# Attention scores as two 64-row matmuls per pair of heads, issued by pairs, with the middle blocks unrolled

## What is computed

```python
sc = jnp.einsum("bhrqd,bhrkcd->bhrqkc", qg, kb) * (hd ** -0.5)       # A: 4 heads, 8 x 16 neighbourhood
sc = jnp.where(col_valid[:, None, :], sc + bias, NEG_INF)
p = jax.nn.softmax(sc.reshape(b, h, rows, GRID_W, kr * GRID_W), axis=-1)
...
o, lse = banded_attention(q, k, v, half_w, slopes, dilation, sink)   # B: 6 heads, +-128 tokens, sink
...
for window, d in ((128, 1), (512, 4), (2048, 16)):                   # C: 6 heads, three dilations,
    o, lse = banded_attention(to_sub(q), to_sub(k), to_sub(v), ...)  #    merged by their denominators
```

## Time and profile before

| what | value |
|---|---|
| median of 3 runs | 2898.84 us (2894.78 to 2903.01) |
| span of the profiled execution | 2891.3 us |
| PE busy | 2779.0 us, 96% |
| DVE busy | 1347.7 us, 47% |
| ACT busy | 862.7 us, 30% |
| granted TensorE clock, mean | 0.989 of full |
| attention, first layer | 287.6 to 605.5 us |
| attention, second layer | 1717.6 to 2035.6 us |

### The profile page before, as it was taken

The page is one execution under the profiler, slowest core; times in us unless marked ns, Lnnn a source line. Parts: engine busy times, 40 slices in busy tenths (PEclk is TensorE's granted clock), DMA queues, the critical chain, the costliest instruction groups (busy, mean ns, idle before and its releaser), DMA issues.

```text
span 2891.3 us, 38682 instructions
## 1 busy us (share of the span) xinstructions
PE 2779.0 (96%) x13768; PEld 2299.5 (80%) x13768; DVE 1347.7 (47%) x2898; ACT 862.7 (30%) x1688; POOL 152.3 (5%) x254
## 2 busy tenths in 40 slices
PE   5999999989999999999989999999899999999998
PEld 5877888777888888888878778878778888888886
DVE  4377666663233333333434776666542333333333
ACT  3222655543211111111032236555441111111110
POOL 2000311100000000000000003111000000000000
PEclk9999999999999999999999999999999999999999
DMA  5211600021111111111041125000212111111111
GB/s 161 77 44 48 155 30 12 17 94 44 57 46 51 44 51 51 44 51 44 0 138 44 44 81 125 19 18 12 104 33 66 51 44 51 44 50 46 48 37 58
DMA packets 212196, 161.44 MB, mean 56 GB/s; under 512 B 52976, under 2 KB 190192, under 8 KB 212080
## 3 DMA queue, kind: packets, MB, share of 16 engines
q1 hardware_dynamic: 204176, 159.93, 18.4%
q10 hardware_dynamic: 7904, 0.04, 0.2%
HBM read 137.27 MB, written 22.66 MB: 55 GB/s over the span
## 4 chain that ended last, share of the span: by engine, by line
PE 45%; DVE 3%; ACT 1%; issue 1%; DVEq 0%; POOL 0%; POOLq 0%; ACTq 0%
PE psum L1433 11%; PE psum L1435 11%; PE psum L1434 11%; PE psum L1519 4%; PE psum L1555 3%; PE psum L1535 2%; PE psum L1484 1%; PE psum L1449 1%; ACT UH L325 0%; DVE X L1313 0%; DVE XN L947 0%; DVE GL L1303 0%; DVE TA L1192 0%; DVE GT L1300 0%; DVE T L1044 0%
## 5 line engine op out<-in xcount | busy, mean ns | idle before, releaser
L1433 PE MATMUL psum<-HH,UH 128*128 128x512 f32 x1856 | 743.1, 400 | 1.3 <-ACT VB L725 1.3
L1435 PE MATMUL psum<-HH,UL 128*128 128x512 f32 x1856 | 723.0, 390 | 0.0
L1434 PE MATMUL psum<-HL,UH 128*128 128x512 f32 x1856 | 723.0, 390 | 0.0
L329 DVE TENSOR_TENSOR UL<-UR,UH 128x1024 fp32r<-128x1024 f32 x116 | 142.0, 1227 | 852.3 <-ACT UH L325 852.3
L1433 PEld LDWEIGHTS psum<-HH,UH 128*128 128x128 f32 x1856 | 348.5, 188 | 86.7 <-issue 12.0
L1434 PEld LDWEIGHTS psum<-HL,UH 128*128 128x128 f32 x1856 | 348.5, 188 | 83.4 <-issue 12.0
L1435 PEld LDWEIGHTS psum<-HH,UL 128*128 128x128 f32 x1856 | 348.4, 188 | 72.7
L1313 DVE TENSOR_TENSOR X<-X,psum 128x512 f32<-128x512 f32 x352 | 236.0, 685 | 147.4 <-PE psum L1435 146.7
L1433 PE MATMUL psum<-PH,GH 128*128 128x512 f32 x704 | 276.0, 392 | 3.0 <-DVE X L1313 3.0
L1434 PE MATMUL psum<-PL,GH 128*128 128x512 f32 x704 | 274.1, 389 | 0.0
L1435 PE MATMUL psum<-PH,GL 128*128 128x512 f32 x704 | 274.0, 389 | 0.0
(11 more groups left out here) (143 smaller groups left out, 3168.3 us busy)
## 6 DMA issues: line engine op xcount, KB each, us to landing
UR<-in_w_gu SPq DMA_DIRECT2D x176, 256.0 KB, 3.1
PR<-in_w_down SPq DMA_DIRECT2D x88, 256.0 KB, 2.9
UR<-in_w_in SPq DMA_DIRECT2D x56, 256.0 KB, 3.2
x_res<-X SPq DMA_DIRECT2D x2, 4096.0 KB, 13.5
PR<-in_w_out SPq DMA_DIRECT2D x32, 256.0 KB, 4.5
X<-x_res SPq DMA_DIRECT2D x2, 4096.0 KB, 14.2
G<-g_d SPq DMA_DIRECT2D x32, 198.0 KB, 2.5
VR<-v_c SPq DMA_DIRECT2D x16, 390.0 KB, 3.6
```

What stands on the lines that cost most here:

```text
L329: nc.vector.tensor_tensor(UL[:, slot, :, :], UR[:, slot, :, :], UH[:, slot, :, :].bitcast(F32), ALU.subtract).then_inc(unit_lo, 1)
L1433: t.matmul(dst, sh, mh, start=start, stop=False)
L1434: t.matmul(dst, sh, ml, start=False, stop=False)
L1435: return t.matmul(dst, sl, mh, start=False, stop=stop)
```

## The change

- `score` becomes `score_pair`: the scores of tiles s and s + 1 are issued together. Each multiplies over 64 rows only, the lower half of the partitions for the first head and the upper half for the second, for each 512 columns first one and then the other.
- The score of a tile goes to bank `s % 4`, a single bank, so that four tiles are held. Exceptions: the first c3 stage uses banks 0 and 2, and tiles 12 to 15 of a block keep the two-bank slots.
- `score_free` says which reads must be finished before a pair is issued.
- `pe_body` goes in steps of two tiles: both scores of s + 2 and s + 3, all transposes of s and s + 1, the weighings of s - 2 and s - 1. The programs of the other engines keep their order.
- The four `mid` blocks are four entries of the plan, without a loop.

```diff
-            for kind, rounds, b0 in (("c3", 2, 0), ("c2", 2, 0), ("b0", 1, 0), ("b1", 1, 1), ("mid", 4, 2),
-                                     ("b6", 1, 6), ("b7", 1, 7)):
+            for kind, rounds, b0 in (("c3", 2, 0), ("c2", 2, 0), ("b0", 1, 0), ("b1", 1, 1), ("mid", 1, 2), ("mid", 1, 3),
+                                     ("mid", 1, 4), ("mid", 1, 5), ("b6", 1, 6), ("b7", 1, 7)):
...
-                    elif dilated(entry[0]):
+                    else:
                         program(entry[0], shifted(entry, 1), before)
                         program(shifted(entry, 1), after, entry[0])
-                    else:
-                        program(entry[0], shifted(entry, 1), before)
-                        with loop(eng, 1, rounds) as r:
-                            program(shifted(entry, r), shifted(entry, r + 1), shifted(entry, r - 1))
...
+            def score_out(bd, s):
+
+                k = bd["kind"]
+                if k == "c3" and bd["i"] == 0:
+                    return bank[2 * (s % 2)]
+                if not dilated(bd) and s >= 12:
+                    return score2[s % 2]
+                return bank[s % 4]
+
+            def score_free(bd, s):
+
+                k = bd["kind"]
+                if k == "c3" and bd["i"] == 0 or not dilated(bd) and s >= 12:
+                    return bd["T"] + s
+                if s < 4:
+                    return bd["T"] - 1 + s // 2
+                return bd["T"] + s - 2
...
-                    tt, sc = T[:, s % 4, off:off + w], score2[s % 2][:, 0:w]
+                    tt, sc = T[:, s % 4, off:off + w], score_out(bd, s)[:, 0:w]
...
-                def score(bd, s):
+                def score_pair(bd, s):
+
                     if s % 6 == 0:
                         pe.wait_ge(staged, bd["Q"] + 2 * (s // 6 + 1))
                         if dilated(bd):
                             pe.wait_ge(staged_low, bd["G"] + s // 6 + 1)
-                    slot = s % 2
-                    if needed(bd["T"] + s - 1):
-                        pe.wait_ge(tmin_s, bd["T"] + s - 1)
-                    for j, kk in enumerate(keys(bd, s)):
-                        w = kk.shape[-1]
-                        last = t.matmul(score2[slot][:, 512 * j:512 * j + w], QS[:, s % 12 if dilated(bd) else s, :], kk, start=True, stop=True)
-                    last.then_inc(scored, 1)
+                    if needed(score_free(bd, s)):
+                        pe.wait_ge(tmin_s, score_free(bd, s))
+                    for j in range(len(keys(bd, s))):
+                        for par in range(2):
+                            rows = slice(64 * par, 64 * par + 64)
+                            kk = keys(bd, s + par)[j]
+                            w = kk.shape[-1]
+                            last = t.matmul(score_out(bd, s + par)[:, 512 * j:512 * j + w],
+                                            QS[rows, (s + par) % 12 if dilated(bd) else s + par, :], kk[rows],
+                                            start=True, stop=True)
+                            if j == len(keys(bd, s)) - 1:
+                                last.then_inc(scored, 1)
...
-                    for s in range(nt):
+                    for s in range(0, nt, 2):
                         if s + 2 < nt:
-                            score(bd, s + 2)
+                            score_pair(bd, s + 2)
                         elif nxt is not None:
-                            score(nxt, s + 2 - nt)
+                            score_pair(nxt, 0)
                         for idx, ev in enumerate(evs):
-                            if ev[0] == s:
+                            if ev[0] in (s, s + 1):
                                 unit(bd, idx, ev, bd["i"] - 1)
-                        if s >= 2:
-                            weigh(bd, s - 2)
-                        elif prev is not None:
-                            weigh(prev, n_tiles(prev) + s - 2)
+                        for e in range(2):
+                            if s >= 2:
+                                weigh(bd, s - 2 + e)
+                            elif prev is not None:
+                                weigh(prev, n_tiles(prev) + s - 2 + e)
```

More of the change, by code:

```diff
@@ L1562, in pe_body @@
                     nt = n_tiles(bd)
-                    for s in range(nt):
+                    for s in range(0, nt, 2):
                         if s + 2 < nt:
-                            score(bd, s + 2)
+                            score_pair(bd, s + 2)
                         elif nxt is not None:
-                            score(nxt, s + 2 - nt)
+                            score_pair(nxt, 0)
                         for idx, ev in enumerate(evs):
-                            if ev[0] == s:
+                            if ev[0] in (s, s + 1):
                                 unit(bd, idx, ev, bd["i"] - 1)
-                        if s >= 2:
-                            weigh(bd, s - 2)
-                        elif prev is not None:
-                            weigh(prev, n_tiles(prev) + s - 2)
+                        for e in range(2):
[3 more added lines that the diff above has]
+                                weigh(prev, n_tiles(prev) + s - 2 + e)
                 pe.wait_ge(qk_s, 2 * QT - 2)
-                score(plan[0][0], 0)
-                score(plan[0][0], 1)
+                score_pair(plan[0][0], 0)
                 run(pe, pe_body)
```

## The result

The changed kernel takes 3017.6 us (3010.7 to 3035.1) against 2898.8 us. The ratio is 1.042, with a 95% interval of 1.039 to 1.045: 119 us slower, in the forecast direction, 1.6 times the forecast 74 us and at the upper edge of the range. It is the page of the profile after that shows what was missed. These are its lines for the span, the busy times and the granted clock of TensorE by slice (tenths of full speed).

A forecast was written before the change was run, and what follows sets the result against it. PE was taken to bound c2 and the blocks, its hand-over with DVE the first c3 stage. Per layer 8.3 + 3 + 1.5 + 24.4 = 37.2 us, +74 in all, gave 2973 us; range 2870 to 3020.

The forecast's parts named there:

- What bounds the kernel: PE's own instructions in c2 and the blocks; in the first c3 stage the hand-over between PE and DVE.
- Part 1: Score pairs: three pass times instead of four, or the load floor if longer; 0.76 to 0.85 us at 192 before visits.
- A, A, B, B: Two passes per head, lower then upper half, starting in program order; only the middle two could lie side by side.
- my load floor: In a score pair, four weight loads one after another need 3 x 0.108 us ahead of the last pass.
- R2: Rival: halves and weight loads side by side, a pair 0.36 + 2p; net -11 us per layer, 2877 us, chance 0.17.
- Part 2: Every score pair enters and leaves 64-row work: 0.36 us a visit, low end 0.28, high 0.4.
- Part 3: Waits of the pair order at wide tiles, first c3 stage and staging; a mid block +3.4 us, first c3 +8.3.
- my row of terms: Mid block, start of pair 12/13 to start of pair 14/15: scores, transposes, copies and reads, put at 5.6 us.
- the signs I had named: PE share well below 96%, idle before scores for DVE's reads, first c3 stage about 31 us, mid blocks about 34.
- All with the clock as now: Granted clock assumed unchanged in every case; more idle PE in c3 could add a few us, held by the range.
- R1: Rival: full overlap of the passes (2p) with the same waits; +23 us per layer, 2945 us, chance 0.23.
- Parts 4 and 5: Four banks remove no wait worth naming; unrolling the mid blocks is worth 0 to 0.2 us a block, counted 0.

The follow-up runs named there:

- e10: e7 with its pairs over all 128 rows, order and four banks kept: 2896.3 us, 1.000 of the kernel before.
- e3: The changed kernel with every score over all 128 rows, its order, banks and waits kept: 3005.0 us, 1.038 of the kernel before.
- e8: The changed kernel with the scores of both c3 stages over all 128 rows, order kept: 3003.2 us, 1.036 of the kernel before.
- e4: The changed kernel with c3 and c2 as before (full rows, one score at a time, old slots), pairs in the blocks alone: 2936.5 us, ratio 1.014.
- e1: The kernel before with its four mid blocks written out, nothing else: 2895.8 us, ratio 0.9997.
- e12: e7 with b0 one score at a time over full rows: 2882.7 us, 0.995 of the kernel before.
- e9: The changed kernel with its first c3 stage in the old order over full rows: 3024.7 us, 1.043 of the kernel before.
- e7: e4 with transposes and weighings interleaved in the blocks, and tiles 12 to 15 one at a time over full rows: 2878.6 us, ratio 0.994.
- e2: The kernel before, mid blocks written out, each score over 64 rows but one at a time in old order and slots: 3498.9 us, ratio 1.208.
- e11: e7 with c2 as 64-row pairs with four banks too: 2906.9 us, 1.003 of the kernel before.

## Why the prediction came out as it did

**What bounds the kernel** was right: PE in c2 and the blocks, the hand-over in the first c3 stage.

**Part 1 (the passes) failed.** I took 3p and loads one after another; it is 2p with the loads side by side (p is one pass, 0.16 us at 192 wide). Two loads of one instant, then two more 0.11 us on, stand in the timeline of the changed kernel as four loads within 0.30 us:

```profile
1795.41 0.30 PEld L1536 LDWEIGHTS psum<-KS,QS 64*128 64x128 f32 x4 [0.69 <-DVE G L1058]
1795.41 0.49 PE L1536 MATMUL psum<-KS,QS 64*128 64x128 f32 x4 [0.50 <-DVE G L1058]
```

Nor is the start order that of the program. A pass of the pair starts ahead of the last 64-row pass of the weighing that was issued before it:

```profile
1868.84 0.43 PE L1536 MATMUL psum<-KS,QS 64*128 64x192 f32 x1
1868.99 0.27 PE L1575 MATMUL psum<-VR,PT 64*128 64x65 f32 x1
1869.10 0.54 PE L1536 MATMUL psum<-KS,QS 64*128 64x192 f32 x3
```

So my reason, that A, A, B, B in program order leaves only the middle two side by side, has no ground on this chip. The Trainium skill, "TensorE: Matmul & The Clock Gate" (Part 3), is borne out where it says that row groups run concurrently; where it says that matmuls keep program order at their starts, these three lines differ, and the measurement decides. At full clock 384-wide pairs take 0.85 us from the first pass to the first transpose, under both 1.3 (3p) and 1.0 (2p with my load floor). R2, which I gave 0.17, had the passes and the loads right, and its waits wrong.

**Part 2 (a visit)** was at its low end: 2p + 0.28, with 0.07 us ahead of the first pass, gives 0.60 us at 192 (0.53 + 0.07), 0.71 at 256 and 0.92 at 384. I had taken 0.36, which the 0.06 us behind the pair (e10) nearly makes good: with it a visit costs some 0.35.

**Part 3 (the waits)** holds in the main, by e3: the first c3 stage +8.8 and +7.9 us (forecast +8.3), the second +3.1 (+3), the two c2 stages +2.0 and about +2.8 (together +1.5), a mid block +4.6 (the waits alone were put at 2.0 + 0.4 + 0.8 + 0.4 + 0.5 = 4.1). The agreement in c3 is partly luck: e3's first stage is at a clock of 0.57 and 0.62, which I hadn't counted, and my figure for the second held the pair's own cost too, which e3 doesn't have. In a mid block, from PE's timeline of the changed kernel:

```profile
537.12 0.70 PE L1536 MATMUL psum<-QK,QS 64*128 64x256 f32 x4
...
539.10 0.41 PE L1555 MATMUL psum<-ident,T 128*128 128x128 f32 x2 [0.69 <-DVE PT L1194]
...
540.55 1.30 PE L1536 MATMUL psum<-QK,QS 64*128 64x512 f32 x8
...
545.24 1.30 PE L1536 MATMUL psum<-QK,QS 64*128 64x512 f32 x8 [1.17 <-DVE G L1058]
```

S(12) to S(14) takes 4.69 us against 3.65, with the wait for tile 13's read where I put it: +1.0, not +2.0. The pair ahead is 0.6 us cheaper (1.23 us to the first transpose, not 1.80), and my row of terms adds up to 5.44 us and not to 5.6; what is left, 0.15 us, would be DVE's links. S(14) to S(0) is 549.41 - 545.24 = 4.17, +0.1 (+0.4 forecast). S(10) to S(12) is 3.43 against 2.98, +0.4 as forecast, but what PE waits for is the bank of a transpose, not the read of tile 11. The blocks, forecast at +24.4 us a layer, come to +0.2 to +1.3 each where the clock is full, and b7 to +2.6 (forecast +2.5): 8 us a layer. Most of the error is the cheaper pair, for with 2p I had put a mid block at +1.3, which comes to +0.8, and the blocks of a layer at +10. Of the signs I had named, the waits for DVE's reads came (25.2 us in all, by the view of waits), but PE's share stayed at 95%, the first c3 stage took 29.5 us for 31 and a mid block 31.4 for 34.

**The clock is the term that was mis-sized, and the step that failed most.** The prediction held it as before ("All with the clock as now") and gave it "a few us, which the range holds", and only for waits in c3. Where one stage stands at both levels the difference can be read: c2 43.95 to 27.4 us (e8), b0 29.9 and 31.5 to 19.4 (e4), b5 37.4 to 31.4. Over both layers: first c2 stages 18, b0 23, b4 and b5 10. The second c2 stages have no run of the same kernel at full clock; against their 31.1 us of before plus the 2.8 of e3 they give 12 and 9. The second c3 stages against e3's 20.7 give 11; these last two are estimates across kernels. That is about 80 of the 123 us. So the sum came out at 1.6 times the forecast by two errors of opposite sign: blocks forecast some 17 us a layer too dear, the clock missing with 40. R1's sum (2p, the same waits), 2945 us, and 80 us of clock would be 3025 us, against 3017.6.

**What goes before a fall** can be read. Up to the last score of each attention part, every fall of the clock in the profiles of these kernels comes during a wait of PE or within 3 us behind one, the longest wait there being of 0.6 to 1.9 us; the one exception is the second c2 stage of e8's first layer. Many such waits are of the pair order. The changed kernel's second c2 stage in the second layer falls at 1884.6 us, behind the first of these rows; e3, with full rows, has the same wait in that stage (second row) and falls 1.1 us behind it. Before there was no wait for POOL there.

```profile
1884.47 0.95 PE L1536 MATMUL psum<-KS,QS 64*128 64x192 f32 x4 [1.60 <-POOL KS L1393]
```
```profile
1856.92 0.89 PE L1536 MATMUL psum<-KS,QS 128*128 128x192 f32 x4 [1.61 <-POOL KS L1393]
```

What differs is how long it lasts: 10.2 us in e3, 64.9 in the changed kernel. Outside the first c3 stage no fall under full-row scores alone lasted over 10.2 us (e1, e3, e10, e12); with 64-row scores they lasted from 3.4 us to over 100 (e8, e9). So in these kernels the fall goes with a wait, and the rows bear on how long it lasts.

**Parts 4 and 5** were right: four banks alone are worth nothing (e10), unrolling nothing (e1).

**What stays open:** why one wait is followed by a fall and the same wait in the other layer isn't, and so whether a given c2 stage loses the clock. The first c2 stage of the changed kernel was at half clock in the first layer and mostly not in the second, and in e8 the other way about. How long a fall lasts under 64 rows isn't explained either: b0 left it after 1.6 us in one layer of e7 and after 24.6 in the other. The first c3 stage is at half clock in all kernels with the pair order there, with 64 rows or 128, so its +6 us holds both waits and clock; they weren't separated.

## What to carry to other kernels

Two matmuls over 64 rows on opposite halves do run side by side, loads included, at 2p plus some 0.3 us for going there and back; this pays where the passes are long (384 wide: 0.92 us for 1.40), and by the same sum not at 128 (0.21 + 0.35 for 0.55). But count the clock with it: before such a change, read the granted clock of each stage, and expect that a fall to 1.2 GHz behind a wait of a us or two can last through whole stages once the scores are on 64 rows. So the waits are to be taken out first. Issuing in pairs costs its waits wherever two buffers are all there is: pair only the tiles with four banks, and keep other PE work between two uses of one bank (e7: 0.994 of the kernel before).

## What the hardware showed that I had not expected

- PE busy for 50.60 of 50.60 us at a granted clock of 0.50, for whole stages, where the scores are 64-row passes one at a time (e2); busy share doesn't say that the clock is full.
- The half clock can outlast its cause under 64-row pairs: b0, entered at it, stayed there for 22 to 31 us (after, e4, e8, e9, e11, and one layer of e7), but in the other layer of e7 for 1.6; wide tiles did so too, 27.3 us from the end of b4 into b5 (e4). The first c3 stage of the earlier trace rows had 3.4 us of it and left.
- The clock falls behind waits of 0.6 to 1.9 us, with full rows as with 64 (e3 and after: the same 1.6 us for POOL's KS).
- Passes on different halves of the array can start in another order than they are issued in (1868.84 ahead of 1868.99 us above).
